# Identity matmuls added to each step of the last attention, from its fifth group on

## The reference

```python
m_out = memory_attention(mq, mk, mv)                              # 4 heads of 64, 256 memory rows
y = sliding_window_attention_with_sinks(q, shared_k, shared_v, sinks[b])   # 12 heads of 64, window 128
mixed = jnp.concatenate([y, m_out], axis=-1) @ w_out[l]
h = h + rms_norm_2(mixed, norm_mix_post[l])
f = swiglu_ffn(rms_norm_2(h, norm_ffn_pre[l]), w_ffn_in[l], w_ffn_out[l])
h = h + rms_norm_2(f, norm_ffn_post[l])
```

## Time and profile before

| | us |
|---|---|
| median of 3 runs | 2070.89 |
| the three runs | 2064.46, 2070.89, 2752.97 |
| the profiled execution's own time | 2063.23 |
| span of the profiled execution | 2061.4 |
| TensorE busy in it | 1951.0 (95%) |
| VectorE busy | 1158.6 (56%) |
| ScalarE busy | 1027.6 (50%) |
| mean granted TensorE clock | 0.987 |

### The profile page before, as it was taken

The page is one execution under the profiler, slowest core; times in us unless marked ns, Lnnn a source line. Parts: engine busy times, 40 slices in busy tenths (PEclk is TensorE's granted clock), DMA queues, the critical chain, the costliest instruction groups (busy, mean ns, idle before and its releaser), DMA issues.

```text
span 2061.4 us, 40794 instructions
## 1 busy us (share of the span) xinstructions
PE 1951.0 (95%) x16470; PEld 1713.9 (83%) x16470; DVE 1158.6 (56%) x1793; ACT 1027.6 (50%) x1624; POOL 156.4 (8%) x151
## 2 busy tenths in 40 slices
PE   7999999899999999999999999999889998999997
PEld 5884588787888788788788899999889998778997
DVE  4421588654543343364355667567767646767654
ACT  5333478544431232354555456455666645366653
POOL 0000100001000000100253210010020001010000
PEclk9999999899999999999999999999999999999999
DMA  8431278432333333332100156664437654225653
GB/s 262 111 118 41 67 233 276 148 96 82 92 92 92 92 100 94 85 103 82 42 4 4 57 162 195 184 184 138 129 96 207 184 177 133 82 72 154 187 175 107
DMA packets 441800, 254.55 MB, mean 123 GB/s; under 512 B 10816, under 2 KB 440512, under 8 KB 441536
## 3 DMA queue, kind: packets, MB, share of 16 engines
q1 hardware_dynamic: 441664, 252.59, 41.4%
HBM read 251.51 MB, written 1.05 MB: 123 GB/s over the span
## 4 chain that ended last, share of the span: by engine, by line
PE 82%; DVE 10%; ACT 4%; issue 2%; DMA 2%; SPq 0%; POOL 0%; DVEq 0%; ACTq 0%; POOLq 0%
PE bank L380 21%; PE bank L381 21%; PE bank L382 20%; PE bank L372 2%; DVE weights_lo L330 2%; PE bank L601 2%; PE bank L602 2%; ACT weights_hi L323 1%; DMA ring<-ada_w 1%; PE bank L1992 1%; PE bank L941 1%; PE bank L399 1%; DVE h L2619 1%; PE bank L609 1%; PE bank L2017 1%
## 5 line engine op out<-in xcount | busy, mean ns | idle before, releaser
L330 DVE TENSOR_TENSOR weights_lo<-ring,weights_hi 128x1024 fp32r<-128x1024 f32 x472 | 578.3, 1228 | 358.4 <-ACT weights_hi L323 353.6
L323 ACT ACTIVATE weights_hi<-ring 128x1024 fp32r<-128x1024 f32 x472 | 495.6, 1054 | 379.5 <-PE bank L382 356.7
L380 PE MATMUL bank<-x_hi,weights_hi 128*128 128x256 f32 (+1 forms) x2024 | 637.2, 315 | 28.4 <-DVE x_lo L2575 11.1
L381 PE MATMUL bank<-x_lo,weights_hi 128*128 128x256 f32 (+1 forms) x2024 | 627.0, 310 | 0.0
L382 PE MATMUL bank<-x_hi,weights_lo 128*128 128x256 f32 (+1 forms) x2024 | 627.0, 310 | 0.0
L380 PEld LDWEIGHTS bank<-x_hi,weights_hi 128*128 128x128 f32 x2024 | 379.8, 188 | 63.1 <-issue 24.1
L381 PEld LDWEIGHTS bank<-x_lo,weights_hi 128*128 128x128 f32 x2024 | 379.8, 188 | 23.7 <-issue 1.4
L382 PEld LDWEIGHTS bank<-x_hi,weights_lo 128*128 128x128 f32 x2024 | 379.8, 188 | 23.1
L380 PE MATMUL bank<-hidden_hi,weights_hi 128*128 128x256 f32 (+1 forms) x864 | 270.6, 313 | 5.7 <-DVE hidden_lo L2896 3.2
L381 PE MATMUL bank<-hidden_lo,weights_hi 128*128 128x256 f32 (+1 forms) x864 | 270.7, 313 | 0.0
L382 PE MATMUL bank<-hidden_hi,weights_lo 128*128 128x256 f32 (+1 forms) x864 | 269.3, 312 | 0.0
(11 more groups left out here) (358 smaller groups left out, 2272.5 us busy)
## 6 DMA issues: line engine op xcount, KB each, us to landing
ring<-mlp_w SPq DMA_DIRECT2D x128, 512.0 KB, 3.9
ring<-ada_w SPq DMA_DIRECT2D x96, 512.0 KB, 4.7
ring<-w_ffn_in SPq DMA_DIRECT2D x88, 512.0 KB, 3.8
ring<-w_ffn_out SPq DMA_DIRECT2D x32, 512.0 KB, 3.5
ring<-gdn_w_in SPq DMA_DIRECT2D x24, 512.0 KB, 3.8
ring<-even_w_in SPq DMA_DIRECT2D x18, 512.0 KB, 4.1
ring<-w_out SPq DMA_DIRECT2D x16, 512.0 KB, 3.9
ring<-w_in_a SPq DMA_DIRECT2D x14, 512.0 KB, 3.7
```

Source lines behind the costliest of these rows:

```text
L323: nc.scalar.activation(w_hi[:, g % AHEAD, :], ring[:, g % RAW, :], ACT.Copy).then_inc(hi_done[g % AHEAD].sem, 1)
L330: nc.vector.tensor_tensor(w_lo[:, g % AHEAD, :], ring[:, g % RAW, :], w_hi[:, g % AHEAD, :].bitcast(F32), ALU.subtract).then_inc(lo_done[g ...
L380: pe.matmul(dst, lhs[0](k), rhs[0](k), start=start and k == 0, stop=False)
L381: pe.matmul(dst, lhs[0](k), rhs[1](k), start=False, stop=False)
```

## The change

In each step from `i` = 4 to the last one with scores, three `keep_busy` matmuls into bank 4 stand between the scores of group `i` and the transposes of group `i-2`. The first attention of the second block uses the same class but has only four groups, so the condition never holds there. The last attention has 14 groups: ten steps, thirty matmuls of 128x128 on 128x256 in float32, in bank 4.

```diff
                     if i == 2:
                         keep_busy(pe, 1, 10)
+                    if 4 <= i < self.n:
+                        keep_busy(pe, 4, 3)
                     if 0 <= i - 2 < self.n:
                         j = i - 2
                         g, (to, _) = self.groups[j], self.turned(j)[0]
```

## The result

| | before | changed |
|---|---|---|
| median of 22 runs, us | 2066.07 | 2072.71 |
| lowest, highest | 2057.19, 2752.97 | 2064.95, 2084.74 |
| ratio of the runs | | 1.0037, 95% interval 1.0024 to 1.0051 |
| the profiled execution's span | 2061.4 | 2071.7 |

The change makes the kernel slower by 0.37%, 7.6 us by the ratio (5.0 to 10.5), well inside 2%. The one run of 2752.97 is not in the ratio. The forecast was 10.7 us, and 2075 us as the time.

The account below looks back on a forecast made before the run. TensorE, with 82% of the chain of waits, was taken as the bound once matmuls were added: 12.9 us of work less 2.08 hidden, taken as 10.7, on a base near the low runs gave 2075 us, range 2067 to 2086.

Parts of the forecast that it names:

- The price of a matmul: Last attention, TensorE: each added matmul costs 0.43 us at the full clock, three in a step 1.29, ten steps 12.9.
- What is hidden: Before the transposes, steps 5 to 14: added matmuls use up 2.08 us of TensorE's waits for VectorE; no other wait opens.
- Step 4: First added set: 2.58 us at the lower level, pushing transposes and values behind the clock's return, so net 1.29 us.
- The sum: Whole last attention: 12.9 - 2.08 = 10.8 us slower, 10.65 stepping through the pieces, taken as 10.7.
- its own case: The forecast itself, last attention: 9.4 to 12.9 us slower, given 0.62.
- the rival in which it pays: Last attention: the clock returns 7.7 and 4.2 us, so 2069.7 us and not slower; chance 0.13.
- The section: Scores of step 4 to first matmul of the projection's remainder: from 41.0 us to 51.7.
- Hidden work: Last attention: VectorE the true bound, transposes waiting in every step, nearly all cost vanishes, 2063 to 2066 us; chance 0.03.
- a longer low stretch: Past step 5: the clock's return slips, each further half-speed step takes 3.95 us more, two give 2081.8; chance 0.12.
- an early return within step 4: Step 4: denser work brings the clock back sooner, cost only 8.9 to 9.1 us, 2072; chance 0.10.
- The base: Starting time for the whole kernel: 2063.23 us profiled, runs 2064.46 and median 2070.89; the low end favoured, giving 2075.

Follow-up runs that it names:

- only4: Kernel before with three added matmuls in step 4 only: section from the scores of step 4 to the projection's remainder 42.48 us against 41.01, ratio to before 1.0004.
- fill_plus: The change's three matmuls in each of steps 4 to 13, plus matmuls filling the gaps of steps 2 and 3: section 49.16 us, ratio to before 1.0028.
- fill: Kernel before with two more matmuls in step 2 and four in step 3, none in steps 4 to 13: section 38.31 us, ratio to before 0.9972.
- After_third: The changed kernel, unaltered, timed and traced once more against before: section 51.82 us, ratio to before 1.0046.
- from5: Kernel before with three added matmuls in each of steps 5 to 13, none in step 4: section 48.02 us, ratio to before 1.0045.

## Why the prediction was right

- **The price of a matmul.** 0.43 us and 1.29 a set; measured 0.433 apart from the first of a set. A set took 1.40 us from its start to the transposes, which then took 0.53 for 0.59, so 1.34 in all. That is 0.05 a step more than the sum had.
- **What is hidden.** 2.08 us of waits, all used up, none opened in their stead: TensorE busy for 33.59 of 33.59 us. The step came to 4.00 us for 3.95 forecast. (VectorE's 1.70 us in that reasoning are 1.72 by its rows; nothing hangs on it.)
- **Step 4.** A set at the lower level takes 2.73 us (2.58 forecast), and only4 shows the net of 1.3 to 1.5 us. The transposes of that step still ran at the lower level (0.99 us), not behind the clock's return as forecast; only the values came behind it, and the price of the step hangs on the low time alone. The prediction let the clock come back at the same moment; against the scores of step 4 it came back 0.6 us later in the first trace of the change, which costs 0.3 us.
- **The sum.** 10.7 forecast, 11.03 in the trace's section, 10.85 between fill_plus and fill, 7.6 (5.0 to 10.5) in the runs' ratio. The work was sized rightly, and the difference of the traces at the full clock, 10.7 to 10.9, is its best measure. The runs are lower than the trace by 3 us, and their 7.6 lies below the 9.4 to 12.9 that the prediction gave for its own case; at equal mean clock two hours of later runs give 11.3 and 11.4. So the difference lies probably in the clock, a term that the prediction set to nothing from a single trace, with 0.13 for the rival in which it pays. For the first runs this is argued and not shown, since those of before have no clock beside them.
- **The section** was to be 51.7 and is 52.04.
- **The rivals.** Hidden work falls by the closed waits; a longer low stretch by the 10.2 us or less in all three traces of the change; as for an early return within step 4, in none of the six traces with added matmuls in step 4 and a low stretch did the clock come back less than 5.5 us after the scores of step 4 began (5.5 to 6.8; before 5.5 and 5.8). After_third is no such case, though it was low for 6.8 us only: its clock fell later, at 1789.2, with the transposes of step 3 behind it, and came back at 1796.0, 5.5 us after those scores, as before:

```profile
1788.29 0.66 PE L2764 MATMUL bank<-tables,arena 128*128 128x128 f32 x4 [1.94 <-DVE arena L2801]
1790.51 2.07 PE L2750 MATMUL bank<-arena 64*128 64x256 f32 x4
```

```profile
1789.00:1790.00 1.00, 1.00 (x7) 1.00 (x8) 0.79 (x3) 1.00 (x4) 0.19 (x1) 0.60 0.00 0
1796.00:1797.00 1.00, 1.00 (x10) 0.85 (x8) 0.00 (x0) 0.74 (x2) 0.19 (x1) 0.99 0.00 0
```

- **The other rival and the base.** The rival in which the clock pays back 11.9 us (7.7 and 4.2), making the change no slower, falls; a part of it, some 2 us, stays open. The base was mistaken by a little: the early median of 2070.89 stood for a kernel whose median over 22 runs is 2066.07, and taking a value between it and the profiled time was right. That 2075 came within 2.3 us of 2072.71 is in part luck: the base taken, 2064.3, was 1.8 us too low, and the cost 4.1 us above the 6.6 by which the medians differ. And a difference far under 2% can be told: with 22 runs each the interval is 1.0024 to 1.0051.

## What to carry to other kernels

Work that does nothing belongs where the engine waits anyway: four identity matmuls in a wait of 1.94 us (and, in all traces but one, more in the wait before it) cost nothing and took a stretch at half clock away, while thirty in steps with only 2 us of waits cost 0.43 us each beyond those, and won back no more than some 2 us that may be chance. Before such work is added, read two things beside each other: the waits in brackets of the engine that is to be kept busy, and where in time the granted clock falls. Here it fell between the start of the wait of step 3 and 1.5 us behind its end, and matmuls added in step 4 came too late to change that. Where the clock's low stretches wander from run to run, compare a section of the trace that holds the change, or runs at equal mean clock, ahead of the whole time.

## What was not expected of the hardware

In the ten traces with the gaps unfilled the low stretch behind them has one of three lengths, 3.4, 6.8 or 10.2 us, though the code up to there is the same. In from5 the clock came back 3.4 us after it fell, at the start of step 4, up to which its code is that of before, where the clock stayed low for 10.2. So the instructions alone do not settle how long it stays low; what else does, these traces do not say. And over the runs, a mean clock that is 0.001 lower goes with 1.6 us more. An estimate from this: 0.001 of mean clock is 4.1 us at the lower level, of which up to 2.07 us could be lost; 1.6 suggests that about three quarters of the low time lies under work that counts.
